# Norms issued behind their own tile's products, attention paced with weights, and new priorities in a list-scheduled two-layer decoder trunk

## The chip, the cores and the metric

The kernel runs on the 8 cores of one Trainium2 chip. Each core computes two of the 16 sequences, all cores run the same program, and they do not exchange data. The metric is the device time of the slowest core in microseconds (us). Within a core, TensorE (PE in the profile) does the matrix products, VectorE (DVE), ScalarE (ACT) and GpSimd (POOL) the element-wise work, and SyncE (SP) issues DMA transfers.

## The reference

`x` is 16 sequences of 2048 positions and 1024 channels. Cut to what matters:

```python
h = x
# layer 0
xn = rmsnorm(h, g0)
a, xb, gate_b, gate_c = split(xn @ ab_w_in)              # 512 columns each
mix = concat(pool_mixer(a), gate_b * conv3(gate_c * xb)) # windows 2/4/8/16; depthwise width 3
h = h + mix @ ab_w_out
h = h + square(relu(rmsnorm(h, g0m) @ w1_0)) @ w2_0      # 1024 -> 4096 -> 1024
# layer 1
xn = rmsnorm(h, g1)
u, v = split(gelu(xn @ cd_w_in[:, :1024]))
c = u * (W_s @ layernorm(v) + b_s)                       # causal, chunks of 128 positions
q, k, val = split(xn @ cd_w_in[:, 1024:])                # 8 heads of 64
z = q @ k.T / 8                                          # strictly causal
d = (sigmoid(z) * suffix_product(1 - sigmoid(z))) @ val  # stick-breaking, no softmax
h = h + concat(c, d) @ cd_w_out
h = h + square(relu(rmsnorm(h, g1m) @ w1_1)) @ w2_1
out = rmsnorm(h, gf)                                     # rmsnorm: h / sqrt(mean(h*h) + eps) * g
```

## The kernel before

**Tiles and stages.** Activations lie transposed, channels on partitions. A unit is 1024 positions of a sequence, in two halves t = 0, 1 of 512. F(s,u), for unit u of sequence s, is layer 0: an input projection of 16 weight blocks, pooling and convolution, an output projection of 8 blocks, an MLP of 64. M(s,u) is the first part of layer 1: gating (V, then U) and the projections to values, keys and queries. S(s,u) is the rest of it: output projection, MLP, final norm. The order is F(0,0) M(0,0) F(0,1) M(0,1) S(0,0) F(1,0) M(1,0) F(1,1) M(1,1) S(0,1) S(1,0) S(1,1).

**Groups.** A *group* (line 627) is eight products 128x512 that add up in one of three PSUM banks; another instruction then empties the bank: `evac_h` (line 701) adds it to the residual h on VectorE and squares the sum on ScalarE into the buffer X_45; in an MLP's first layer (W1) ScalarE does relu in the bank and then the square out of it. An MLP has four quarters: W1, W2, W1, W2.

**A norm** (line 640) of one half sums the eight squared tiles by eight products with a matrix of ones (in the profile `ps<-X_45,cbs`), in a first part of six when six tiles are squared and a second of two. ScalarE then does Ln (L651) and Exp (L655), and VectorE eight normalisations of 128x512 (L665), which write over the squares in X_45. The next stage's products read those. The norms after an output projection are spawned when all its 16 groups have been issued, those after layer 0's MLP when that MLP has been issued. `prefetch_x` (line 718) loads, squares and normalises the next unit's x into a second buffer, X_44, during the MLP before it.

**Attention** (lines 1161 to 1252) runs beside the other stages. An *item*, a query block of 128 by up to 512 keys, is two score products (L1206) into one of two pairs of PSUM banks, a sigmoid on ScalarE, two VectorE scans (L1217), a copy of the carry to the next item of the chain (L1225), a GpSimd difference (L1231) and a transposing transfer (L1244, Wk<-Wq) on SP's queue. After four items, eight value products follow (L1275). Items are released in proportion to `main_t`, the count of main products issued, over a window `win` set in `build`.

**Weights.** A ring of ten blocks is loaded on GpSimd's queue in the order that `block_order` lists (line 556). The first use of a block loads and converts f32; `keep_block` (line 595) then stores a bf16 copy from SP's queue, which later uses load. This falls on F(0,0), M(0,0) and the 72 blocks of S(0,0), the first tail pass.

**What sets the order.** All work is written as fibers that yield instructions, pool requests and conditions; a planner puts them in a fixed order per engine before the kernel runs. It takes the instruction with the smallest modelled start plus two biases, so a negative bias is an urgency:

```python
r = f.req
st = S.ready(r)
k = (st + f.bias + r.bias, f.n)
```

An engine then runs its instructions in that order. `hcount` makes an output projection wait until all eight tiles of a half's h are being loaded. `finbusy` holds a half while its final norm still uses mix as staging; the input groups of F wait for it.

## Time and profile before

| | us |
|---|---|
| median of 3 runs (lowest, highest) | 3035.44 (3034.34, 3356.67) |
| the profiled execution's own time | 3030.56 |
| its span on the slowest core (all cores) | 3029.0 (2994.9 to 3029.0) |
| TensorE busy | 2859.8 (94%) |
| VectorE, ScalarE, GpSimd busy | 1413.3, 1411.9, 1180.1 |

The profile is of one execution on its slowest core; times count from the start of the span. The clock column is TensorE's granted clock as a share of full speed, the mean over a stretch. The wait that the profile names ahead of an instruction is what ended the engine's idle time.

### The profile page before, as it was taken

What the parts mean: (1) busy time and instruction counts of PE and PEld (TensorE: products, weight loads), DVE (VectorE), ACT (ScalarE), POOL (GpSimd) and SP (SyncE); (2) the same over time, 40 slices, a digit from 0 to 9 for tenths busy, and PEclk for the clock granted to TensorE, in tenths of its full rate; (3) what the DMA queues carried; (4) which work ended last, traced back from release to release, by engine and by line L of the source; (5) the groups of instructions that cost most, each with busy time, mean ns of one, the idle gap of its engine ahead of it and who ended that gap; (6) DMA issues with size and microseconds to landing.
All of it is one profiled execution on the core that took longest, in us unless ns stands there. A gap on an engine that the chain in (4) does not pass through costs nothing.

```text
span 3029.0 us, 43342 instructions; the slowest of 8 cores (2994.9 to 3029.0 us)
## 1 busy us (share of the span) xinstructions
PE 2859.8 (94%) x13365; PEld 1215.2 (40%) x13365; DVE 1413.3 (47%) x1671; ACT 1411.9 (47%) x2398; POOL 1180.1 (39%) x1685
## 2 busy tenths in 40 slices
PE   8999989999989899899998999998999989999998
PEld 3344433344433334334343334443344434443443
DVE  3510237443435344883755472433555574644002
ACT  2344243556446344356454345444564556453442
POOL 4211136343333344653644543433355435641110
PEclk9999999999999899899999999999999989999999
DMA  7778972455867997754676253565356584755222
GB/s 160 174 171 181 195 201 72 122 114 126 200 175 121 158 174 151 189 134 107 147 165 183 73 108 96 118 145 174 79 117 125 101 219 109 135 113 171 83 77 84
DMA packets 456912, 420.18 MB, mean 139 GB/s; under 512 B 310256, under 2 KB 334960, under 8 KB 456688
## 3 DMA queue, kind: packets, MB, share of 16 engines
q1 hardware_dynamic: 387424, 228.46, 32.5%
q0 software_dynamic: 69264, 188.95, 29.1%
q8 instruction: 114, 1.87, 0.3%
q14 instruction: 110, 0.90, 0.1%
HBM read 304.20 MB, written 89.13 MB: 130 GB/s over the span
## 4 chain that ended last, share of the span: by engine, by line
PE 80%; DVE 6%; DMA 4%; POOL 3%; issue 3%; ACT 3%; SPq 1%; DVEq 0%; POOLq 0%; ACTq 0%
PE ps L550 76%; PE ps L1206 3%; DVE X_45 L665 2%; PE ps L1275 2%; DVE P L1217 1%; DMA Wk<-Wq 1%; DMA ring<-wblk 1%; POOL Wq L1231 1%; DMA h<-xT 1%; POOL ps_77 L934 1%; POOL ps_74 L934 1%; SPq L1244 0%; SPq L543 0%; DMA stg<-xT 0%; ACT ms L655 0%
## 5 line engine op out<-in xcount | busy, mean ns | idle before, releaser
L550 PE MATMUL ps<-X_45,ring 128*128 128x512 bf16 x4864 | 1107.0, 384 | 22.3 <-DVE X_45 L665 20.8
L540 ACT ACTIVATE ps<-ps 128x512 f32<-128x512 f32 (+3 forms) x832 | 575.5, 697 | 554.6 <-PE ps L550 323.6
L550 PEld LDWEIGHTS ps<-X_45,ring 128*128 128x128 bf16 x4864 | 469.6, 99 | 617.7 <-issue 90.1
L1231 POOL TENSOR_TENSOR Wq<-P 128x1022 bf16<-128x1022 f32 (+2 forms) x320 | 527.3, 1648 | 421.2 <-DVE P L1217 401.7
L550 PE MATMUL ps<-mix,ring 128*128 128x512 bf16 x2816 | 659.1, 380 | 3.9 <-DVE mix L905 3.0
L1217 DVE TENSOR_TENSOR_SCAN P<-ps,carry,cbs 128x512 f32<-128x512 f32 x384 | 486.7, 1276 | 244.5 <-ACT ps L540 233.4
L583 POOL DMA_DIRECT2D ring<-wbf x540 | 296.3, 550 | 778.6 <-PE ps L550 699.0
L706 DVE TENSOR_TENSOR h<-ps,h 128x512 f32<-128x512 f32 x384 | 263.2, 687 | 626.5 <-PE ps L550 623.2
L550 PE MATMUL ps<-ffB,ring 128*128 128x512 bf16 x2048 | 483.8, 379 | 0.0
L1217 DVE TENSOR_TENSOR_SCAN P<-ps,cbs 128x128 f32<-128x128 f32 (+3 forms) x256 | 208.1, 819 | 508.7 <-ACT ps L540 496.6
L550 PEld LDWEIGHTS ps<-mix,ring 128*128 128x128 bf16 x2816 | 262.1, 98 | 337.0 <-issue 44.2
L540 ACT ACTIVATE X_45<-h 128x512 bf16<-128x512 f32 x256 | 160.7, 628 | 393.1 <-DVE h L706 392.9
L550 PE MATMUL ps<-X_44,ring 128*128 128x512 bf16 x1280 | 297.9, 389 | 12.4 <-DVE X_44 L665 5.8
L550 PEld LDWEIGHTS ps<-ffB,ring 128*128 128x128 bf16 x2048 | 200.4, 98 | 241.7
L583 POOL DMA_DIRECT2D ring<-wblk x180 | 98.2, 553 | 368.8 <-PE ps L550 336.5
L550 PEld LDWEIGHTS ps<-X_44,ring 128*128 128x128 bf16 x1280 | 123.7, 100 | 170.8 <-issue 38.5
L540 ACT ACTIVATE mix<-ps 128x512 bf16<-128x512 f32 x288 | 171.8, 597 | 33.2 <-PE ps L550 7.6
L540 ACT ACTIVATE ffB<-ps 128x512 bf16<-128x512 f32 x256 | 152.8, 597 | 23.9 <-ACT ps L540 0.4
L665 DVE SCALAR_TENSOR_TENSOR X_45<-h,cfs,ms 128x512 bf16<-128x512 f32 x192 | 141.3, 807 | 31.2 <-ACT ms L655 31.2
L550 PE MATMUL ps<-ring,X_45 128*128 128x512 bf16 x512 | 127.6, 399 | 27.6 <-DVE X_45 L665 14.5
L1206 PE MATMUL ps<-kT,qT 64*128 64x512 bf16 (+3 forms) x640 | 112.1, 359 | 17.9 <-DVE P L1217 17.8
L1225 ACT ACTIVATE carry<-P 128x2 f32<-128x2 f32 x192 | 37.9, 199 | 125.7 <-DVE P L1217 124.8
(112 smaller groups left out, 1331.3 us busy)
## 6 DMA issues: line engine op xcount, KB each, us to landing
ring<-wbf POOLq DMA_DIRECT2D x540, 256.0 KB, 3.9
ring<-wblk POOLq DMA_DIRECT2D x180, 256.0 KB, 6.9
wbf<-ring SPq DMA_DIRECT2D x180, 256.0 KB, 5.4
stg<-xT SPq DMA_DIRECT2D x96, 256.0 KB, 4.6
h<-xT SPq DMA_DIRECT2D x64, 256.0 KB, 7.0
hsp<-h SPq DMA_DIRECT2D x64, 256.0 KB, 5.0
h<-hsp SPq DMA_DIRECT2D x64, 256.0 KB, 7.0
oT<-mixf SPq DMA_DIRECT2D x32, 256.0 KB, 7.1
```

The costliest lines, as they stand in the source:

```text
L540: return Req("act", lambda e: e.activation(out=out, in_=in_, func=func, **kw), reads, writes, dur, bias=bias)
L550: ins = pe.matmul(out, lhsT=l, rhs=r, start=(first and i == 0), stop=(last and i == n - 1), skip_group_check=True)
L583: yield Req("pool", (lambda slot, b, src: lambda e: e.dma_start(out=self.ring[:, slot, :], in_=src[b]))(slot, b, src), ([self.Lwbf[b]] if ...
L665: yield Req("dve", lambda e: e.scalar_tensor_tensor(out=X[:, c, ts], in0=self.h[:, c, ts], scalar=g, in1=m, op0=ALU.mult, op1=ALU.mult), [ ...
L706: yield Req("dve", lambda e: e.tensor_tensor(out=self.h[:, c, ts], in0=self.bank(bk), in1=self.h[:, c, ts], op=ALU.add), [], [self.Lbank[b ...
L934: yield Req("pool", (lambda src, d, b0: lambda e: e.tensor_tensor(out=S1[:, b0:528][:, ::-1], in0=src[:, b0:528][:, ::-1], in1=src[:, b0 - ...
L1206: ins = pe.matmul(zt[:, h * 512:h * 512 + w], lhsT=self.qT[hp, a, il * 128:(il + 1) * 128], rhs=self.kT[hp, a, k0:k0 + w], start=True, sto ...
L1217: yield Req("dve", (lambda h: lambda e: e.tensor_tensor_scan(out=P[:, h, 0:w][:, ::-1], data0=zt[:, h * 512:h * 512 + w][:, ::-1], data1=f ...
L1225: yield Req("act", lambda e: e.activation(out=self.carry[:, cy, :], in_=P[:, :, 0:1].rearrange("p h o -> p (h o)"), func=AF.Copy), [LP], [ ...
L1231: yield Req("pool", lambda e: e.tensor_tensor(out=W3[:, :, 0:w - 1], in0=P[:, :, 1:w], in1=P[:, :, 0:w - 1], op=ALU.subtract), [LP], [LWq] ...
L1275: ins = pe.matmul(av[h * 64:(h + 1) * 64, r0 * 128:512], lhsT=lhsT, rhs=rhs, start=(first and j == 0), stop=(c == 0 and j == 3), skip_grou ...
```

## The change

1. *Norms.* `out_proj` spawns the norms of both halves before its groups, and `stage_F` those of layer 0's MLP before the MLP, so that a norm can stand in the order as soon as its tiles are squared.
2. *Stage M.* The order V, U, values, K, Q becomes V, U, K, values, Q, in the code and in `block_order`. K and Q take one block at a time, V and values four.
3. *Pacing.* Items are released by `pace_t`, which counts a group in F's input projection as 0.4 and in S's output projection as 0.2 of a full one; the windows in `build` are shortened to match.
4. *Biases.* Ln and Exp -0.7, normalisations -1.0, `evac_h` -1.2, sigmoid -0.3, carry copy -1.0; an attention item's fiber 0.0 instead of 0.4, the final norm's -0.6 instead of 0.1.
5. *Conditions.* h loads are counted per tile (`hload`); `finbusy` is asked by the two instructions that write mix, not by the input groups.
6. `keep_block` is unchanged: S(0,0) stores the copies of its 72 blocks as before.

The diff, cut to its core; the lines that begin with # name the place:

```diff
+PACE = 0.4
+PACEO = 0.2
     # block_order, kind "M"
-                seq(B_V, 20)
+                seq(B_V, 8)
+                seq(B_K, 4)
+                seq(B_VV, 4)
+                seq(B_Q, 4)
...
     # group
         self.main_t += n
+        self.pace_t += n * self.pace_w
...
     # norm: Ln and Exp
-            [self.Lcf], [self.Lms[ms], self.Lbank[bk]], 1.9)
+            [self.Lcf], [self.Lms[ms], self.Lbank[bk]], 1.9, bias=-0.7)
...
     # to_X: X_45 <- h * g * m
-                [self.Lh[c][t], Lm, self.Lcf], [LX[c][t]], 0.75)
+                [self.Lh[c][t], Lm, self.Lcf], [LX[c][t]], 0.75, bias=-1.0)
...
     # evac_h: h <- bank + h
-                      [], [self.Lbank[bk], self.Lh[c][t]], 0.70)
+                      [], [self.Lbank[bk], self.Lh[c][t]], 0.70, bias=-1.2)
...
     # chain_conv gb, and chain_pool ahead of its ACTIVATE mix<-ps
-            yield lambda: "y" in st
+            yield lambda: "y" in st and t not in self.finbusy
...
     # stage_F
+        self.pace_w = PACE
         for i in range(4):
...
-                yield lambda: t not in self.finbusy
...
+        self.pace_w = 1.0
         self.free_x(n)
-        yield from self.out_proj("F", s, u, self.mix, self.Lmix)
         nd = set()
+        yield from self.out_proj("F", s, u, self.mix, self.Lmix, 8, nd)
         ev2 = [[0], [0]]
-        for t in range(2):
-            self.M.spawn(self.norm_h(self.evo[t], t, 8, self.to_X(t, 1), nd), -0.2)
...
-        yield from self.mlp(0, 8, nd, ev2, then)
...
         for t in range(2):
             self.M.spawn(self.norm_h(ev2[t], t, 16, dst(t), nd2), -0.2)
+        yield from self.mlp(0, 8, nd, ev2, then)
...
     # out_proj
+        evo = [[0], [0]]
+        for t in range(2):
+            self.M.spawn(self.norm_h(evo[t], t, gcol, self.to_X(t, 1), nd), -0.2)
         for t in range(2):
-            yield lambda: (self.mixn[t] == 8 if kind == "F" else (s, u, t) in self.mready) and \
-                self.hcount.get((kind, s, u, t)) == 8
+            yield lambda: self.mixn[t] == 8 if kind == "F" else (s, u, t) in self.mready
             for c in range(8):
+                yield lambda: (kind, s, u, t, c) in self.hload
...
     # stage_M
+        yield from heads(self.kT, self.LkT, u * UT)
         sl = yield from self.take(4)
         for n in range(8):                      # the eight V groups
...
-        for which in range(2):                  # K, then Q
+        yield from heads(self.qT, self.LqT, 0)
...
     # attention
-            yield lambda: self.pace_free or self.main_t >= pace[0] + need * pace[1]
+            yield lambda: self.pace_free or self.pace_t >= pace[0] + need * pace[1]
-            self.M.spawn(self.att_item(s, u, x), 0.4)
+            self.M.spawn(self.att_item(s, u, x), 0.0)
     # att_item: sigmoid bias -0.3, carry copy bias -1.0
...
     # stage_S
+        self.pace_w = PACEO
+        yield from self.out_proj("S", s, u, *src, 24, nd)
+        self.pace_w = 1.0
-            self.M.spawn(self.norm_h(self.evo[t], t, 24, self.to_X(t, 1), nd), -0.2)
...
-            self.M.spawn(fin(t), 0.1)
+            self.M.spawn(fin(t), -0.6)
...
     # build
-        tF, tM, tS = 88 * 16, 20 * 16, 72 * 16
+        tF, tM, tS = (72 + 16 * PACE) * 16, 20 * 16, (64 + 8 * PACEO) * 16
```

Three places in the order of the engines. An `order` row is an engine's next instructions: line, operation, output<-inputs, tile, count. L550 and L552 are the same line before and after, and so are L1206 and L1214, L1057 and L1064, L540 and L542, L651 and L657, L655 and L661.

TensorE at the end of F(0,1)'s output projection (`ps<-mix,ring`) and the start of its MLP (`ps<-X_45,ring`); the norm products are `ps<-X_45,cbs`. Before:

```order
L550 MATMUL ps<-mix,ring 128x512 x24
L1206 MATMUL ps<-kT,qT 128x384 x2
L550 MATMUL ps<-mix,ring 128x512 x16
L550 MATMUL ps<-X_45,cbs 128x512 x16
L1275 MATMUL ps<-Wk,V 64x512 x8
L550 MATMUL ps<-X_45,ring 128x512 x8
L1206 MATMUL ps<-kT,qT 128x512 x2
L550 MATMUL ps<-X_45,ring 128x512 x40
```

And now:

```order
L552 MATMUL ps<-mix,ring 128x512 x24
L552 MATMUL ps<-X_45,cbs 128x512 x6
L552 MATMUL ps<-mix,ring 128x512 x16
L552 MATMUL ps<-X_45,cbs 128x512 x2
L552 MATMUL ps<-mix,ring 128x512 x8
L1214 MATMUL ps<-kT,qT 128x512 x2
L552 MATMUL ps<-mix,ring 128x512 x40
L552 MATMUL ps<-X_45,cbs 128x512 x6
L552 MATMUL ps<-mix,ring 128x512 x8
L552 MATMUL ps<-X_45,ring 128x512 x4
L552 MATMUL ps<-X_45,cbs 128x512 x2
L552 MATMUL ps<-X_45,ring 128x512 x4
```

The first half's norm products now stand among the second half's groups, and the second half's last two behind four products of the MLP.

TensorE at the start of M(0,0): last groups of the MLP (`ps<-mix,ring` and `ps<-ffB,ring`), norms, V (`ps<-ring,X_45`), U (`ps<-X_45,ring`), gating products (`ps<-wmt,vn`). Before:

```order
L550 MATMUL ps<-mix,ring 128x512 x8
L550 MATMUL ps<-ffB,ring 128x512 x8
L550 MATMUL ps<-X_45,cbs 128x512 x16
L550 MATMUL ps<-ring,X_45 128x512 x32
L550 MATMUL ps<-X_45,ring 128x512 x8
L1057 MATMUL ps<-wmt,vn_79 128x128 x4
L1057 MATMUL ps<-wmt,vn_81 128x128 x4
L550 MATMUL ps<-X_45,ring 128x512 x8
L1057 MATMUL ps<-wmt,vn_83 128x128 x4
L1057 MATMUL ps<-wmt,vn_85 128x128 x4
L550 MATMUL ps<-X_45,ring 128x512 x16
L550 MATMUL ps<-ring,X_45 128x512 x32
```

And now:

```order
L552 MATMUL ps<-X_45,cbs 128x512 x6
L552 MATMUL ps<-mix,ring 128x512 x8
L552 MATMUL ps<-ffB,ring 128x512 x8
L552 MATMUL ps<-ring,X_45 128x512 x4
L552 MATMUL ps<-X_45,cbs 128x512 x2
L552 MATMUL ps<-ring,X_45 128x512 x28
L552 MATMUL ps<-X_45,ring 128x512 x32
L1064 MATMUL ps<-wmt,vn_79 128x128 x4
L1064 MATMUL ps<-wmt,vn_81 128x128 x4
L1064 MATMUL ps<-wmt,vn_83 128x128 x4
L1064 MATMUL ps<-wmt,vn_85 128x128 x4
L552 MATMUL ps<-ring,X_45 128x512 x32
```

The first half's gating products stood between its U groups; now they follow its four U groups in one piece.

ScalarE at the end of F(1,0)'s output projection and the start of its MLP: squares (`X_45<-h`), Ln (`ms<-ps,cfs`), Exp (`ms<-ms`), sigmoids (`ps<-ps` of 128x1024 and 128x2x384), squares of the next x (`X_44<-stg`), and of the MLP's first layer relu (`ps<-ps` of 128x512) and square (`mix<-ps`). Before:

```order
L651 ACTIVATE ms<-ps,cfs 128x512
L655 ACTIVATE ms<-ms 128x512
L651 ACTIVATE ms<-ps,cfs 128x512
L655 ACTIVATE ms<-ms 128x512
L1225 ACTIVATE carry<-P 128x2
L540 ACTIVATE ps<-ps 128x2x384
L540 ACTIVATE ps<-ps 128x1024
L540 ACTIVATE X_44<-stg 128x512 x3
L540 ACTIVATE ps<-ps 128x512
L540 ACTIVATE mix<-ps 128x512
L540 ACTIVATE ps<-ps 128x512
L540 ACTIVATE mix<-ps 128x512
```

And now:

```order
L1233 ACTIVATE carry<-P 128x2
L657 ACTIVATE ms<-ps,cfs 128x512
L1233 ACTIVATE carry<-P 128x2
L661 ACTIVATE ms<-ms 128x512
L542 ACTIVATE ps<-ps 128x1024 x2
L542 ACTIVATE ps<-ps 128x512
L542 ACTIVATE mix<-ps 128x512
L542 ACTIVATE ps<-ps 128x512
L542 ACTIVATE mix<-ps 128x512
L657 ACTIVATE ms<-ps,cfs 128x512
L542 ACTIVATE ps<-ps 128x512
L542 ACTIVATE mix<-ps 128x512
```

Before, Ln and Exp of both halves stood in one piece ahead of the MLP; now only the second half's are there, with a copy of a carry between, and the Ln that follows among the MLP's evacuations is that of the next x, whose squares now come earlier.

## Rows read from the trace of the kernel before

**Rows 1.** The page's head and its part 1

```profile
span 3029.0 us, 43342 instructions; the slowest of 8 cores (2994.9 to 3029.0 us)
...
PE 2859.8 (94%) x13365; PEld 1215.2 (40%) x13365; DVE 1413.3 (47%) x1671; ACT 1411.9 (47%) x2398; POOL 1180.1 (39%) x1685
```

**Rows 2.** Waits of TensorE: us in total, times, longest

```profile
PE ps L550 <- DVE X_45 L665: 35.3, 76, 2.1
PE ps L1275 <- DMA Wk<-Wq: 18.1, 2, 13.9
```

**Rows 3.** Timeline of TensorE, F(0,1): start us, us, instruction, count [idle before]

```profile
561.34 3.62 PE L550 MATMUL ps<-X_45,cbs 128*128 128x512 bf16 x16
...
567.02 0.38 PE L550 MATMUL ps<-X_45,ring 128*128 128x512 bf16 x1 [1.07 <-DVE X_45 L665]
567.68 0.38 PE L550 MATMUL ps<-X_45,ring 128*128 128x512 bf16 x1 [0.29 <-DVE X_45 L665]
...
598.68 31.25 PE L550 MATMUL ps<-X_45,ring 128*128 128x512 bf16 x144
```

**Rows 4.** Windows: length; busy us (count) of PE, PEld, DVE, ACT, POOL; clock, DMA

```profile
131.60:155.75 24.15, 21.66 (x89) 8.80 (x88) 11.39 (x17) 12.67 (x21) 0.53 (x1) 0.93 0.46 123
...
2171.39:2199.48 28.09, 24.44 (x104) 9.04 (x103) 19.69 (x24) 17.20 (x27) 9.19 (x9) 0.88 0.30 60
...
364.68:418.19 53.51, 38.87 (x178) 15.64 (x176) 36.33 (x54) 27.28 (x56) 22.73 (x34) 0.94 0.84 205
...
2048.98:2097.54 48.56, 36.60 (x178) 15.73 (x177) 28.61 (x48) 26.19 (x55) 22.68 (x33) 0.96 0.44 137
461.57:531.56 69.99, 63.25 (x300) 26.15 (x299) 55.83 (x65) 25.09 (x41) 51.73 (x84) 1.00 0.29 71
1227.20:1311.99 84.79, 69.99 (x314) 27.94 (x313) 77.37 (x79) 30.89 (x50) 61.87 (x99) 0.90 0.63 165
...
2442.29:2488.97 46.68, 37.78 (x169) 15.54 (x167) 33.95 (x40) 25.38 (x40) 19.20 (x24) 0.89 1.02 262
945.33:1028.69 83.36, 67.92 (x290) 27.18 (x291) 26.11 (x31) 45.15 (x77) 20.62 (x29) 0.86 0.94 148
...
2311.17:2372.16 60.99, 60.99 (x293) 25.73 (x292) 16.96 (x16) 43.46 (x75) 23.71 (x34) 1.00 0.47 108
```

**Rows 5.** Timeline of all engines around the start of M(0,1)

```profile
816.19 3.62 PE L550 MATMUL ps<-X_45,cbs 128*128 128x512 bf16 x16
...
817.25 0.63 ACT L540 ACTIVATE X_45<-h 128x512 bf16<-128x512 f32 x1 [3.43 <-DVE h L706]
...
819.69 5.39 DVE L665 SCALAR_TENSOR_TENSOR X_45<-h,cfs,ms 128x512 bf16<-128x512 f32 x8 [2.54 <-ACT ms L655]
...
839.06 7.75 DVE L665 SCALAR_TENSOR_TENSOR X_45<-h,cfs,ms 128x512 bf16<-128x512 f32 x7
...
840.99 1.61 POOL L1067 TENSOR_TENSOR vt_82<-vt_82,sbias 128x512 f32<-128x512 f32 x1 [0.73 <-ACT vt_82 L1063]
...
867.92 12.46 PE L550 MATMUL ps<-ring,X_45 128*128 128x512 bf16 x57 [2.66 <-DMA ring<-wbf]
```

**Rows 6.** Groups by line and shape: count | busy us, mean ns | idle

```profile
L1231 POOL TENSOR_TENSOR Wq<-P 128x1022 bf16<-128x1022 f32 x224 | 426.4, 1904 | 342.6 <-DVE P L1217 340.6 <-DMA Wk<-Wq 1.1 <-issue 0.2
L540 ACT ACTIVATE ps<-ps 128x512 f32<-128x512 f32 x544 | 316.5, 582 | 340.7 <-PE ps L550 323.6 <-PE ps L1206 16.3
...
L540 ACT ACTIVATE ps<-ps 128x1024 f32<-128x1024 f32 x224 | 224.6, 1009 | 158.0 <-PE ps L1206 157.9
...
L1225 ACT ACTIVATE carry<-P 128x2 f32<-128x2 f32 x192 | 37.9, 199 | 125.7 <-DVE P L1217 124.8
...
L540 ACT ACT_TABLE_LOAD x24 | 30.8, 1283 | 6.7 <-PE ps L550 5.0 <-PE ps L1206 1.4
```

**Rows 7.** Line L1244, the transposes of the attention weights

```profile
DMA to landing us min/median/max: 2.3/4.4/23.2
```

**Rows 8.** Timeline of TensorE in S(0,0)

```profile
1017.41 1.92 PE L1275 MATMUL ps<-Wk,V 128*64 128x512 bf16 x8 [13.86 <-DMA Wk<-Wq]
```

More of the change, by code:

```diff
@@ L652, in norm @@
                                           bias=self.cf[:, 60:61]),
-            [self.Lcf], [self.Lms[ms], self.Lbank[bk]], 1.9)
+            [self.Lcf], [self.Lms[ms], self.Lbank[bk]], 1.9, bias=-0.7)
         self.banks.free(bk)
-        yield Req("act", lambda e: e.activation(out=m, in_=m, func=AF.Exp, scale=-0.5), [], [self.Lms[ms]], 0.63)
+        yield Req("act", lambda e: e.activation(out=m, in_=m, func=AF.Exp, scale=-0.5), [], [self.Lms[ms]], 0.63, bias=-0.7)
         for c in range(8):
@@ L752, in start_x @@
             ts = slice(t * TT, (t + 1) * TT)
-            self.hcount[("F", 0, 0, t)] = 8
+            self.hload.update(("F", 0, 0, t, c) for c in range(8))
             ev = [0]
@@ L784, in load_h_chunk @@
             yield self.load_h(self.hsp, self.Lhsp, s, u, t, c)
-        k = (kind, s, u, t)
-        self.hcount[k] = self.hcount.get(k, 0) + 1
+        self.hload.add((kind, s, u, t, c))
     def free_x(self, n):
@@ L952, in evac @@
                           bias=-1.0, slack=1.0)
+            yield lambda: t not in self.finbusy
             yield Req("act", lambda e: e.activation(out=self.mix[:, g, ts], in_=self.bank(b2), func=AF.Copy,
@@ L1133, in stage_M, with heads @@
         yield from self.need_attention(2 * s + u)
+        def heads(dst, Ldst, d0):
+            for a in range(4):
+                sl = yield from self.take(1)
+                for t in range(2):
+                    ts = slice(t * TT, (t + 1) * TT)
+                    ev = copy_evac(dst[:, a, d0 + t * TT:d0 + (t + 1) * TT], [Ldst[a][d0 // TT + t]], "act")
+                    yield from self.group(self.wpairs(sl[0], X, ts), [self.Lring[sl[0]]] + [LX[k][t] for k in range(8)], ev)
+                self.release(sl[0])
+        yield from heads(self.kT, self.LkT, u * UT)
         sl = yield from self.take(4)
@@ L1140, in stage_M @@
             self.release(x)
-        for which in range(2):
-            for a in range(4):
-                sl = yield from self.take(1)
-                for t in range(2):
-                    ts = slice(t * TT, (t + 1) * TT)
-                    gs = slice(u * UT + t * TT, u * UT + (t + 1) * TT)
-                    if which == 0:
-                        ev = copy_evac(self.kT[:, a, gs], [self.LkT[a][u * 2 + t]], "act")
-                    else:
-                        ev = copy_evac(self.qT[:, a, ts], [self.LqT[a][t]], "act")
-                    yield from self.group(self.wpairs(sl[0], X, ts), [self.Lring[sl[0]]] + [LX[k][t] for k in range(8)], ev)
-                self.release(sl[0])
+        yield from heads(self.qT, self.LqT, 0)
         self.M.spawn(self.attention(s, u), 0.4)
@@ L1179, in attention @@
         acc = 0.0
-        pace = (self.main_t, self.win[(s, u)], tot)
+        pace = (self.pace_t, self.win[(s, u)], tot)
         self.inflight = 0
@@ L1210, in att_item @@
         z3 = zt[:].rearrange("p (h n) -> p h n", h=2)[:, :, 0:w]
-        yield self.act(z3, z3, AF.Sigmoid, [], Lz, 2 * w, True, scale=-0.125)
+        yield self.act(z3, z3, AF.Sigmoid, [], Lz, 2 * w, True, bias=-0.3, scale=-0.125)
         if pv is not None:
@@ L1225, in att_item @@
             yield Req("act", lambda e: e.activation(out=self.carry[:, cy, :], in_=P[:, :, 0:1].rearrange("p h o -> p (h o)"),
-                                                    func=AF.Copy), [LP], [self.Lcarry[cy]], 0.2)
+                                                    func=AF.Copy), [LP], [self.Lcarry[cy]], 0.2, bias=-1.0)
         x["scanned"] = True
@@ L1309, in stage_S @@
         src = (self.mix, self.Lmix) if self.stages[n - 1][0] == "M" else (self.X[0], self.LX[0])
-        yield from self.out_proj("S", s, u, *src)
+        nd = set()
+        self.pace_w = PACEO
+        yield from self.out_proj("S", s, u, *src, 24, nd)
+        self.pace_w = 1.0
         if src[0] is self.X[0]:
             self.free_x(n)
-        nd = set()
         ev2 = [[0], [0]]
-        for t in range(2):
-            self.M.spawn(self.norm_h(self.evo[t], t, 24, self.to_X(t, 1), nd), -0.2)
         nx = self.hnext
@@ L1392, in build @@
         self.main_t = 0
+        self.pace_t = 0.0
+        self.pace_w = 1.0
         self.ffn = [0, 0]
@@ L1399, in build @@
         self.hnext = None
-        self.hcount = {}
+        self.hload = set()
         self.xloading = False
```

5 lines of the change are left out of this document (2 added, 3 removed).

## The prediction

> **What bounds the kernel now.** I read the page's head first: TensorE is busy for 94% of a span of 3029.0 us [rows 1]. Work can therefore become cheaper only where TensorE stands still or runs slowly, and the list of its waits says where: VectorE's normalised tiles X_45 (35.3 us, 76 times), then the transposed attention weights (18.1) [rows 2]. The timeline shows the form of the first. After an output projection come 16 norm products in one piece, then a wait of 1.07 us, then single products 0.66 us apart, as each 128x512 piece of X_45 is written; undisturbed, 144 products take 31.25 us, or 0.216 each [rows 3].
>
> Waits alone understate it, so I priced stretches, window by window [rows 4]: length less its full products at 0.216 us. Attention products in a stretch are cheaper than full ones, so I count them whole for the floor and at nothing for the ceiling.
> - *Output projection to MLP*, eight times, from the first norm product to the 65th MLP product. The first has 88 full products: 24.15 - 19.0 = 5.1 us lost. The dearest (start 2171.39) has 80 full and 24 of attention: 28.09 less 22.5 or 17.3, so 5.6 to 10.8. Counted so, the eight lose 41 to 67; I take 55.
> - *MLP to mixer stage M*, four times, from the norm products to the first product of the K, V or Q projections: 144 full products and 32 of a quarter's width are 32.8 us. The first loses 53.51 - 32.8 = 20.7, the last 48.56 - 32.8 = 15.8, all four 73.
> - *Input projections of F(0,1), F(1,0), F(1,1)*: 264 full products, 57.0 us. F(0,1) loses 5.2 to 13.0 (I take 9), F(1,1) is like it (8), F(1,0) loses 17.0 to 27.8 (22).
> - *Output projection of S(1,0)*: 46.68 us, 144 full products, 10.2 to 15.6 lost (13).
>
> The granted clock averages 0.88 in the dearest handoff and 0.90 in F(1,0)'s input: after such gaps part of the products run at the lower level (1.2 GHz). A whole quarter of an MLP without gaps holds 1.00 (2311.17) [rows 4]. The windows contain that loss, so it is not added again. Together these places lose 180 us.
>
> **The change, part by part.**
> *Norms behind their own products.* Count of instructions is unchanged; 12 pairs of norms move. The first half's norm now stands among the second half's products, and the second half's last two norm products stand four products into the next stage (the order rows). For the first half the whole chain is hidden by 6 groups of 8 products or more, 10.4 us. For the second half I read the chain where it is seen alone: from the end of the products (816.19) the last square ends at 817.88, 1.7 us later; the norm products took 8 x 0.216 of the 3.5 us to the first normalisation at 819.69, so Ln and Exp need 1.8; eight normalisations take 5.39 [rows 5]. That is 1.7 + 0.4 + 1.8 + 5.4 = 9.3 us, under the next 64 products' 13.8. What stays: TensorE takes its instructions in order, so the two norm products wait for that square: 1.7 - 4 x 0.216 = 0.8 us; and behind Ln and Exp ScalarE does a table load and a sigmoid (1.28 and 1.01 [rows 6]) before it empties the first bank, which I put at another 1.2. Left: 8 x 2 = 16 of 55, gain **39** (25 to 58). The eight h loads that each M norm lets go, and the final norm's stores, issue earlier on SP's queue; nobody on TensorE waits for them there.
> *M stage.* The same 0.8 us, then the four gating products of the first half stand behind all its U products (before: between them) and need four banks, of which three exist: the fourth waits for ScalarE's four scalings, and so does the next V group. From the rows' durations I count about 4 us there and 3 to 4 at the second half's gating products. The VectorE block of second-half normalisations that ran beside the gating (7.75 us for seven) is out of the way, and K, taken one block at a time, replaces V, which needed four blocks at once and cost a wait of 2.66 us on the ring [rows 5]. On POOL's queue the loads stand no earlier, but only K's third block waits for them, 6.9 us later than V did. Left: 9 each, 36 of 73, gain **37** (13 to 57).
> *Pacing.* Input projections of F now count 0.4, output projections of S 0.2. In the order, F(0,1)'s input has 5 attention items instead of 9, F(1,0)'s 7 instead of 12, S(1,0)'s output 2 instead of 7. VectorE was busy 77.37 of 84.79 us in F(1,0)'s input [rows 4], which I take for the reason of the loss; I halve it there: gain **19** (9 to 29). In S(1,0)'s output seven items become two; gain **9.5** (5 to 13).
> *Where the items go.* Mostly into the W1 quarters of the MLPs (each MLP is W1, W2, W1, W2): the order has 170 scores in them instead of 93, up to 17 in one (F(1,0)'s first). That quarter then asks of ScalarE 64 evacuations at 0.58 (37 us), 17 sigmoids (17), about 13 carries at 0.20 (3) and, as the norm of the next x tile falls into the same place, four table loads (5) and two norms' Ln and Exp (at most 1.8 each by the rows above, 4): 66 us, against 55.3 of products and some 8 of attention's. So this one quarter is ScalarE-bound by a few us; the others, with 11 to 16, ask up to about 60 of 62. In the row without loss (2311.17, nine scores) ScalarE asked 43.46 of 60.99. Cost **8** (0 to 40).
> *Tail pass.* S(0,0) still stores the weight copies. Its first quarter goes from 9 to 14 scores, and there the transposes landed up to 23.2 us late against a median of 4.4, one value product waiting 13.86 us [rows 7, 8]; that quarter lost 83.36 - 290 x 0.216 = 20.7 us at a DMA share of 0.94 [rows 4]. Cost **6** (-18 to +40).
> *At nothing:* loads of h counted per piece only relax a condition that no wait of TensorE names. The condition that the final norm has left mix moves from the input groups to the two writers of mix; a writer that waits keeps one of three banks, and the groups behind it stop after two more. I take nothing, since the final norms now rank ahead of all else there; without that cover it would be the rest of eight normalisations, 5.4 us, at the one place where F follows S.
>
> Sum: 39 + 37 + 19 + 9.5 - 8 - 6 = 90.5. The profiled execution took 3030.56, so 2940; the median of the runs shown is 3035.44, 4.9 above it, so **2944 us**.
>
> **A rule against it.** The seven normalisations beside GpSimd's additions (840.99) took 1.11 us each, the eight without 0.67 [rows 5]. With 1.11 the second half's chain is 3.9 + 8.9 = 12.8 us, still under 13.8, and the sum stands. If instead each of the eight waited out one whole GpSimd difference (1.90 us [rows 6]), the chain would be 3.9 + 5.4 + 15.2 = 24.5, 10.7 late in six handoffs that now have attention beside them: 64 us given back. The Trainium skill has such a rule ("SBUF — State Buffer", Who interferes with whom): a VectorE instruction with two SBUF inputs and a GpSimd one that reads SBUF exclude each other, and the later is fully blocked. The rows agree that there is a cost, and show 0.44 us of it.
>
> **Rivals.**
> 1. *The second half's normalisations late* (just worked out): 2944 + 64 = 3008. It begins to cost at 4.5 us, 0.56 per instruction. For: POOL's differences move into that stretch. Against: the order puts two or three scores beside them, so two or three differences, not eight.
> 2. *ScalarE paces the denser quarters.* If half of each of 170 sigmoids (1.01 us [rows 6]) delays a bank, 170 x 0.5 = 85 us less the 8 counted: about 3021. For: 66 us asked of a quarter of 63 in F(1,0). Against: three banks leave 3.5 us between a group's end and the need for its bank.
> 3. *Slower: value products wait in the tail pass.* S(0,0) holds 12 of them, TensorE takes them in order, and one such wait with its slow products cost about 15 us (the 20.7 less the 5.9 that the handoff in it loses by the same count). Six more give the whole gain back; all 12 give 2944 + 11 x 15 = 3109. For: more transposes in a quarter with a DMA share of 0.94. Against: the pass holds 53 scores instead of 51, so the load is shifted, not raised.
> 4. *More goes away:* the residues at their least and the 18.1 us of transpose waits too: about 2897.
>
> That the change does nothing is excluded by the order.
>
> **Numbers.** Forecast 0.56 (2915 to 2974); rival 4 0.15; rival 1 0.08; rival 2 0.09; rival 3 with six or more waits 0.06; two to four more waits (about 2990 to 3010) 0.06. A difference of 2%, 61 us, is about what a measurement of this kernel can tell from none: below 2975 is faster (0.71), up to 3096 the same (0.24), above slower (0.05). The range 2895 to 2997 leaves out the slow end of rivals 1 to 3.
>
> **What would show it.** Right: X_45 waits of TensorE under 12 us; the eight handoffs at most 3 us over their products; from M's first to its 129th full product near 39 us; F(1,0)'s input near 73; S(1,0)'s output near 36. Wrong: waits for ScalarE's emptied banks in the first MLP quarters, value products waiting for transposes more than twice in S(0,0), or that stretch of M over 44 us.

## The result, and the profile after

The changed kernel takes **2965.93 us** (median of 4 runs, 2964.73 to 2966.79) against 3034.34 for the kernel before in the same job: a ratio of 0.9773, 95% interval 0.9754 to 0.9792. The prediction was 2944 with 2895 to 2997 as its range, so the time lies inside, with 68 us gained where 90.5 had been summed. In some executions the cores of one die run at a lower granted clock and take longer; all times here are medians of the other executions, and the kernels without stores and with the late final norm, which have one of these each, have no ratio.

The page's head and part 1 of the kernel after, beside [rows 1]:

```profile
span 2964.9 us, 43355 instructions; the slowest of 8 cores (2927.3 to 2964.9 us)
...
PE 2836.3 (96%) x13361; PEld 1210.1 (41%) x13361; DVE 1401.7 (47%) x1671; ACT 1416.4 (48%) x2408; POOL 1180.4 (40%) x1685
```

TensorE's waits (us in total, times, longest), beside [rows 2]:

```profile
PE ps L552 <- DVE h L712: 17.6, 9, 5.0
PE ps L552 <- ACT X_45 L542: 15.2, 15, 4.1
PE ps L1283 <- DMA Wk<-Wq: 9.6, 3, 7.1
```

The 35.3 us of waits for normalised X_45 tiles are gone. What is left of the norm is its last two products, which wait for the last square (15 times). At the top stands a wait that the kernel before does not have: for a bank that is not emptied, because `evac_h` waits for h.

The handoff of F(0,1), where [rows 3] had a wait of 1.07 us and eight single products 0.66 apart:

```profile
543.55 1.75 PE L552 MATMUL ps<-X_45,cbs 128*128 128x512 bf16 x6
...
546.88 1.03 PE L552 MATMUL ps<-X_45,ring 128*128 128x512 bf16 x4
548.78 0.59 PE L552 MATMUL ps<-X_45,cbs 128*128 128x512 bf16 x2 [0.87 <-ACT X_45 L542]
549.21 1.03 PE L552 MATMUL ps<-X_45,ring 128*128 128x512 bf16 x4
```

The wait of 0.87 us is the 0.8 that the prediction worked out from the square's end; the MLP's first eight products run without any other. The windows that answer to [rows 4] have the same columns (length; busy us and count of PE, PEld, DVE, ACT, POOL; clock; DMA share; GB/s). They are, in this order: M(0,0) from its first product to K's first, the inputs of F(0,1) and F(1,0), S(1,0)'s output, and F(1,0)'s first W1 quarter:

```profile
362.90:402.20 39.30, 33.78 (x163) 15.15 (x162) 20.85 (x37) 22.48 (x50) 18.36 (x28) 0.92 0.80 214
444.80:513.90 69.10, 62.49 (x284) 26.09 (x283) 43.04 (x58) 21.15 (x35) 44.85 (x79) 0.98 0.22 63
1187.30:1267.60 80.30, 66.83 (x297) 27.00 (x296) 65.51 (x72) 25.72 (x41) 57.26 (x93) 0.96 0.68 194
2383.20:2428.20 45.00, 35.75 (x150) 14.26 (x149) 30.65 (x40) 20.00 (x30) 12.51 (x16) 0.92 1.00 262
1300.30:1380.60 80.30, 72.77 (x333) 28.48 (x332) 55.98 (x53) 61.87 (x104) 45.52 (x52) 0.94 0.69 132
```

To see where the 64 us between the two spans went, I counted every stretch of both traces alike: its length less its products at 0.216 us per 512 columns, attention's by their width. "Lost" is that difference, on each trace's slowest core.

| stretch | lost before | after | gained | forecast |
|---|---|---|---|---|
| eight handoffs with their first W1 quarter, without value products' waits | 55.7 | 36.4 | 19.3 | 39 - 8 |
| four M stages | 69.1 | 38.9 | 30.2 | 37 |
| inputs of F(0,1), F(1,0), F(1,1) | 34.2 | 36.6 | -2.4 | 19 |
| output of S(1,0) | 11.5 | 13.1 | -1.6 | 9.5 |
| waits of value products in S(0,0) | 18.1 | 9.6 | 8.5 | -6 |
| all else | 5.0 | -4.8 | 9.8 | 0 |
| sum | 193.6 | 129.8 | 63.8 | 90.5 |

(An attention product costs a little less than its width, so a stretch without gaps can come out below nothing. A stage M counts from its first product; the wait for the norm ahead of it, which the prediction counted with M, stands in "all else".)

### The profile page after: what moved, and what is told of

It reads as the page before. It is cut to its first block, busy times and chain, and to the rows that moved or that the text cites. A ratio compares the mean times of both kernels' runs of the same rounds, so it can differ in the third digit from the quotient of the medians.

```text
span 2964.9 us, 43355 instructions; the slowest of 8 cores (2927.3 to 2964.9 us)
## 1 busy us (share of the span) xinstructions
PE 2836.3 (96%) x13361; PEld 1210.1 (41%) x13361; DVE 1401.7 (47%) x1671; ACT 1416.4 (48%) x2408; POOL 1180.4 (40%) x1685
## 4 chain that ended last, share of the span: by engine, by line
PE 84%; DMA 3%; ACT 3%; DVE 3%; issue 3%; POOL 2%; SPq 2%; DVEq 0%; ACTq 0%; POOLq 0%
PE ps L552 79%; PE ps L1214 3%; PE ps L1283 2%; SPq L1252 1%; DMA Wk<-Wq 1%; DMA h<-hsp 1%; POOL ps_74 L939 1%; DMA h<-xT 1%; SPq L545 1%; DVE P L1225 1%; ACT ps L542 1%; DVE h L712 1%; DMA ring<-wblk 0%; ACT vt_80 L1070 0%; POOL ps_77 L939 0%
## 5 line engine op out<-in xcount | busy, mean ns | idle before, releaser
L552 PE MATMUL ps<-X_45,ring 128*128 128x512 bf16 x4864 | 1100.6, 382 | 6.2 <-ACT mix L542 5.4
L542 ACT ACTIVATE ps<-ps 128x512 f32<-128x512 f32 (+3 forms) x832 | 574.1, 697 | 533.4 <-PE ps L1214 289.3
L552 PEld LDWEIGHTS ps<-X_45,ring 128*128 128x128 bf16 x4864 | 463.1, 98 | 583.0 <-issue 71.5
L552 PE MATMUL ps<-mix,ring 128*128 128x512 bf16 x2816 | 659.9, 381 | 3.0 <-ACT ffB L542 1.1
L552 PE MATMUL ps<-ffB,ring 128*128 128x512 bf16 x2048 | 483.8, 379 | 0.0
L552 PEld LDWEIGHTS ps<-mix,ring 128*128 128x128 bf16 x2816 | 264.4, 98 | 337.3 <-issue 42.3
L542 ACT ACTIVATE X_45<-h 128x512 bf16<-128x512 f32 x256 | 159.2, 627 | 378.0 <-DVE h L712 377.6
L552 PE MATMUL ps<-X_44,ring 128*128 128x512 bf16 x1280 | 302.9, 392 | 31.2 <-DVE h L712 15.1
L552 PEld LDWEIGHTS ps<-ffB,ring 128*128 128x128 bf16 x2048 | 200.3, 98 | 241.7
L552 PEld LDWEIGHTS ps<-X_44,ring 128*128 128x128 bf16 x1280 | 124.5, 100 | 195.3 <-issue 65.6
L542 ACT ACTIVATE mix<-ps 128x512 bf16<-128x512 f32 x288 | 171.8, 597 | 49.9 <-PE ps L552 26.9
L542 ACT ACTIVATE ffB<-ps 128x512 bf16<-128x512 f32 x256 | 152.8, 597 | 23.0 <-ACT ps L542 0.7
L552 PE MATMUL ps<-ring,X_45 128*128 128x512 bf16 x512 | 114.7, 383 | 5.0 <-ACT vt_80 L1070 5.0
L1214 PE MATMUL ps<-kT,qT 64*128 64x512 bf16 (+3 forms) x640 | 112.7, 354 | 6.2 <-DVE P L1225 6.0
```

Source lines behind the costliest of these rows:

```text
L542: return Req("act", lambda e: e.activation(out=out, in_=in_, func=func, **kw), reads, writes, dur, bias=bias)
L552: ins = pe.matmul(out, lhsT=l, rhs=r, start=(first and i == 0), stop=(last and i == n - 1), skip_group_check=True)
L1214: ins = pe.matmul(zt[:, h * 512:h * 512 + w], lhsT=self.qT[hp, a, il * 128:(il + 1) * 128], rhs=self.kT[hp, a, k0:k0 + w], start=True, sto ...
```

## Experiments: the norms and the priorities

**Only the norms' place undone.**

```diff
     # out_proj: behind all groups, as before
-        for t in range(2):
-            self.M.spawn(self.norm_h(evo[t], t, gcol, self.to_X(t, 1), nd), -0.2)
         for t in range(2):
...
+        for t in range(2):
+            self.M.spawn(self.norm_h(evo[t], t, gcol, self.to_X(t, 1), nd), -0.2)
```

> The changed kernel with only the place of the norms undone: each norm is spawned behind all 16 groups of the output projection, and behind the whole MLP of layer 0; biases, stage M, pacing stay changed. Theory of the prediction: the norms' place carries the eight handoffs (39 us) and most of what stage M gained (X_45 waits of about 6 us in each of four stages, 24), so about 2966 + 60 = 3026 us, with waits of TensorE for X_45 from VectorE back above 25 us. Rival: the urgency biases do it, since a norm that starts late but is served first loses little: at most 2990.

Measured: 3003.41 us, ratio to before 0.9902 (0.9886 to 0.9919). The place of the norms is worth about 38 us inside the changed kernel, more than half of its gain. The waits for normalised tiles are back, though smaller than in [rows 2]; 5.8 of the 31.8 us is the first wait for x, which every kernel here has:

```profile
PE ps L552 <- DVE X L671: 31.8, 61, 5.8
```

By the count of the table the handoffs lose 23 us more. The expectation's second part fell: the M stages lose only 2.8 us each more, or 3.9 with the quarter ahead of them, where 6 had been expected. More than half of what M gained came from elsewhere (below).

**Only the norms' place changed, on the kernel before.** The edit is the reverse one.

> The kernel before with only the norms spawned ahead of their own groups; order of stage M, pacing, biases and conditions as before. Undoing this in the changed kernel cost 39 us. Theory: the place of the norms is worth about the same alone, 3033 less 35 to 45, about 2993, and TensorE's waits for normalised X_45 tiles fall from 35 us to under 12. Rival: without the urgency biases the norm's Ln, Exp and normalisations stand behind attention's scans and sigmoids, and half of it is lost: 3010 or more.

Measured: 3005.78, ratio 0.991 (0.9878 to 0.9942), about 26 us. Theory and rival were both half right. The waits for X_45 from VectorE are gone, and by the count of the table the stretches gain 59 us; but 32 are given back in one place that nobody had named. The last W2 quarter of S(1,0), in this kernel and, below it, in the changed one:

```profile
2621.20:2729.30 108.10, 75.08 (x361) 30.06 (x360) 75.99 (x76) 41.16 (x63) 55.30 (x61) 0.83 0.81 176
```

```profile
2623.80:2684.70 60.90, 60.90 (x291) 27.02 (x290) 20.85 (x27) 15.25 (x23) 14.39 (x21) 1.00 0.43 94
```

The attention of the last unit is late and has to be finished before S(1,1) can start, so TensorE waits for one item after the other. Two of those waits (idle before in brackets):

```profile
2702.53 0.61 PE L1205 MATMUL ps<-kT,qT 64*128 64x512 bf16 x2 [6.47 <-DVE P L1216]
...
2727.50 1.92 PE L1274 MATMUL ps<-Wk,V 128*64 128x512 bf16 x8 [9.59 <-DMA Wk<-Wq]
```

**All priorities undone, the rest as changed.**

```diff
-            [self.Lcf], [self.Lms[ms], self.Lbank[bk]], 1.9, bias=-0.7)
+            [self.Lcf], [self.Lms[ms], self.Lbank[bk]], 1.9)
...
-            self.M.spawn(self.att_item(s, u, x), 0.0)
+            self.M.spawn(self.att_item(s, u, x), 0.4)
...
-            self.M.spawn(fin(t), -0.6)
+            self.M.spawn(fin(t), 0.1)
```

> The changed kernel with all priorities of before (Ln, Exp, normalisation, evac_h, sigmoid, carry, attention items, final norm). Theory: the priorities are what the early norms need, above all where attention runs beside them, so 15 to 30 us go: 2980 to 2996, in the handoffs of F(0,1), F(1,1), S(0,1), S(1,0). Rival: the place of a norm decides alone and the rest is noise of the order: 2956 to 2972; S(1,0)'s and S(1,1)'s output projections then don't change either, because their h loads, not the final norms, are late.

Measured: 3005.16, ratio 0.9918 (0.9886 to 0.9949): about 40 us lost, more than expected and in other places. The stretches here are of core 0. The handoffs named there lose about what they do in the changed kernel (F(0,1) 0.8 against 3.4, S(0,1) 2.1 against 0.7). The loss is the same pile-up in S(1,0)'s last quarter:

```profile
2616.50:2724.60 108.10, 74.63 (x359) 30.19 (x358) 70.62 (x74) 40.03 (x61) 53.05 (x59) 0.84 0.75 173
```

A smaller one stands in M(1,0), ahead of which the second unit's attention has to end: it loses 30 us instead of 8.9. So the priorities together are worth as much as the norms' place, and without them attention does not keep up with its window. Two kernels with early norms and old priorities show the pile-up, and the kernel before, with late norms, does not (its same quarter loses nothing). My reading is that attention's items then rank behind everything and are left over; which of the priorities matters was not tried. S(1,0)'s output lost only 5.4 here; why is open (below).

## Experiments: pacing and the input projections

**Both weights at 1.0** (`PACE = 1.0`, `PACEO = 1.0`, which also restores the old windows).

> The changed kernel with both weights at 1.0 and so the windows of before: items are released evenly again. Theory of the prediction (VectorE's scans make the input projections long): F(0,1)'s input from 69.1 to about 74, F(1,0)'s from 80.3 to about 88, S(1,0)'s output longer by 8, the first W1 quarter of F(1,0) shorter by 7: about 2986 us. Rival: GpSimd's pooling additions pace the input projections and the h loads S(1,0)'s output, so the pacing is worth nothing there: inputs of F(0,1) and F(1,1) stay within 1.5 us of 69.1, the total between 2960 and 2972.

Measured: 2959.54, ratio 0.9767 (0.9744 to 0.9789). Taking the pacing out costs nothing; the time is 6 us lower, but the intervals overlap, and the mean over the cores is the same (2946.2 against 2946.8). F(0,1)'s input, with nine items again:

```profile
444.60:513.60 69.00, 63.23 (x301) 26.12 (x300) 54.99 (x65) 25.27 (x42) 52.05 (x83) 1.00 0.35 86
```

Against the row of after VectorE has 55 us of work instead of 43, and the stretch is 0.1 us shorter. VectorE's room is not what bounds it. What does, all engines in F(0,1)'s input of the changed kernel:

```profile
462.38 2.18 POOL L588 DMA_DIRECT2D ring<-wbf  x4
...
463.88 0.60 ACT L542 ACTIVATE pa_72<-ps 128x512 f32<-128x512 f32 x1 [1.03 <-PE ps L552]
...
466.10 1.04 POOL L939 TENSOR_TENSOR ps_74<-pa_72 128x518 f32<-128x518 f32 x1
...
467.29 2.23 POOL L939 TENSOR_TENSOR ps_74<-ps_74 128x516 f32<-128x516 f32 x2
...
469.60 1.46 POOL L1239 TENSOR_TENSOR Wq<-P 128x766 bf16<-128x766 f32 x1
469.62 1.98 DVE L948 SCALAR_TENSOR_TENSOR pb_73<-ps_74,pa_72 128x512 bf16<-128x512 f32 x1 [0.75 <-POOL ps_74 L939]
...
471.53 0.68 DVE L891 TENSOR_TENSOR cc_69<-ps,cy_68 128x512 f32<-128x512 f32 x1
...
472.35 0.59 PE L552 MATMUL ps<-pb_73,cbs 128*128 128x512 bf16 x1 [2.39 <-DVE cc_69 L891]
```

Read from the bottom: TensorE waits 2.39 us for a bank that L891 empties; in VectorE's order that stands behind the pooling's L948; that one waits for GpSimd's three additions. GpSimd began them 1.6 us after ScalarE had written their input (pa_72, done at 464.48), behind the issue of four weight loads and three small copies. So the chain runs through GpSimd. Not all of the 2.39 us is its additions, though: L948 took 1.98 us, with a GpSimd difference beside it, where its median is 0.69, and that alone is 1.29.

**The pooling additions on VectorE.**

```diff
-                yield Req("pool", (lambda src, d, b0: lambda e: e.tensor_tensor(
+                yield Req("dve", (lambda src, d, b0: lambda e: e.tensor_tensor(
```

> The changed kernel with the additions of the pooling mixer (20 in each F stage, 1.05 us each on GpSimd) issued to VectorE; nothing is left out. If GpSimd's chain of additions sets the pace of the input projections, F(0,1)'s and F(1,1)'s go from 69.1 to 62 to 65 us, F(0,0)'s from 75 to about 68, the total to about 2945. Rival (VectorE is what is short there): VectorE gets about 14 us more on 43 of 69, the inputs stay at 69 or get longer, the total is 2966 or more.

Measured: 2941.92, ratio 0.971 (0.968 to 0.974), faster than the changed kernel by some 20 us. F(0,1)'s input, with the same five items and without the one group of value products:

```profile
441.10:504.50 63.40, 60.02 (x277) 25.61 (x276) 53.48 (x75) 20.29 (x33) 23.35 (x54) 1.00 0.23 63
```

69.1 became 63.4 (F(1,1): 63.0; F(1,0): 80.3 to 73.5), with VectorE busier and GpSimd at half. By the count of the table F(0,1) loses 5.2 instead of 9.8, F(1,1) 4.7 instead of 9.7, and F(1,0) 13.3 instead of 17.0, there with three items in the order instead of seven. F(0,0)'s input ended only 2.7 us earlier, where 7 had been expected. So the additions on GpSimd made half of the loss in F(0,1) and F(1,1) and less elsewhere. Whether by their length or by what GpSimd's work does to VectorE's instructions beside it, the run does not tell.

**Both at once.**

> Pooling additions on VectorE and both pacing weights 1.0. Theory from the runs so far: pacing is worth nothing in any stage, so the two gains add up: 2942 less 6, about 2936. Rival: VectorE has 55 of 63 us in the inputs now, so with nine items instead of five there it becomes what is late, the inputs of F(0,1) and F(1,1) go from 63 to 67 us and more, and the total to 2950 or more.

Measured: 2949.17, ratio 0.9714 (0.9676 to 0.9753). The gains did not add up. Inputs of 63.8 and 63.4: the rival's 67 did not come either, but the rival was not put to the test, because the planner set six items into these inputs and not nine. By the intervals the kernel cannot be told from the one with the additions alone. By the mean over the cores all its executions (2930.8 to 2941.8) lie above all of that one's (2921.7 to 2928.3), so with the additions out of the way the pacing may be worth some 10 us; where, I did not find out.

## Experiments: the tail pass S(0,0)

On the core shown value products wait 9.6 us there; on core 0 of the same execution one wait is this:

```profile
1034.17 1.92 PE L1283 MATMUL ps<-Wk,V 128*64 128x512 bf16 x8 [18.33 <-DMA Wk<-Wq]
```

On core 1 one wait is 20.6, and core 6 has none. These waits go with a part of the spread of the cores, 2927.3 to 2964.9, and not with all of it: core 6 is the shortest, but core 5, the longest, has 9.6 us of them, and core 1, with 21.9, spans 2947.1.

**No weight copies in the tail passes.** S(0,0) stores none; the later passes load f32.

```diff
-            if b not in self.Lwbf:
+            if b not in self.Lwbf and b < B_L1OUT:
```

> The changed kernel without the bf16 copies of the 72 blocks of the tail passes: S(0,0) stores nothing, and S(0,1), S(1,0), S(1,1) load f32 again, twice the bytes. Theory: the stores in S(0,0) are what makes transposes of attention weights land late there, so its value products no longer wait (9.6 us on the slowest core, 24.6 on core 0) and the cores lie closer together than the 37 us of now: about 2950. Rival: the f32 loads alone fill the DMA engines and the waits stay; or the doubled loads of the later passes make TensorE wait for ring blocks, most of all in S(1,0)'s output projection: 2966 or more.

Measured: 2980.19, ratio 0.9825 (0.981 to 0.9839), slower than the changed kernel by 14. Both sides held in part. On the slowest core S(0,0) still has a value wait of 6.5 us without a single store. But over the eight cores these waits fall from 0 to 24.6 us (mean 13.4) to 0.6 to 6.5 (mean 2.1), so most of the lateness in S(0,0) did come with the stores. What is lost is lost later, as the rival had it. On the slowest core S(0,1), which had no such wait, loses 14.5 in one quarter, where the DMA share is 1.17. The longest wait stands there:

```profile
2233.23 1.92 PE L1283 MATMUL ps<-Wk,V 128*64 128x512 bf16 x8 [10.83 <-DMA Wk<-Wq]
```

Core 7 has 11.0 us of such waits in S(0,1), the other six at most 2.1. S(1,0)'s output loses 20.1 instead of 13.1. So f32 loads without stores can make transposes late too.

**The copies made earlier**, DRAM to DRAM from GpSimd's queue, by a fiber that the code has and did not use:

```diff
+        M.spawn(self.convert(B_L1OUT, 72, 1728, 2300), 0.5)
...
     # convert
+            if b in self.Lwbf:
+                continue
```

> The changed kernel with the 72 weight copies of the tail passes made ahead of need, DRAM to DRAM from GpSimd's queue, spread evenly from the start of F(0,1) to past the middle of S(0,0), which then loads bf16. Theory: the waits for late transposes in S(0,0) (9.6 us on the slowest core, 0 to 24.6 on the others) come from its DMA load, which falls from 0.94 of the engines; they go, the cores' spans lie within 15 us, about 2950. Rival: the same bytes now make transposes late in F(0,1), or 72 more DMA issues lengthen GpSimd's pooling chain there: 2963 or more.

Measured: 2966.05, ratio 0.977 (0.9729 to 0.981), no gain. The first half of the theory is right: on the slowest core S(0,0)'s four quarters lose nothing and no value product waits there, and no core has one of more than 5.1 us there. The rest of it fell, nearly as the rival had it. The last W2 quarter of F(0,1) loses 15.2, and only 3.5 of that is a value product's wait. 8.3 us are norm products that wait for squares; on ScalarE these stand behind the squares of the next x, for whose loads ScalarE waited up to 7.6 us at a time. M(0,1) loses 21.1 instead of 9.9, with a wait for attention's output ahead of S(0,0):

```profile
793.92 0.63 ACT L542 ACTIVATE X<-stg 128x512 bf16<-128x512 f32 x1 [6.57 <-DMA stg<-xT]
...
795.22 2.36 PE L552 MATMUL ps<-X,cbs 128*128 128x512 bf16 x6 [4.26 <-ACT X L542]
...
PE ps L552 <- DMA mix<-dsp: 10.7, 1, 10.7
```

**Value products later in the order**, on top of the additions on VectorE:

```diff
-                  bias=-1.0, slack=4.0)
+                  bias=-1.0, slack=16.0 if (s, u) == (0, 1) else 4.0)
```

> Pooling additions on VectorE, and the value products of the attention that runs beside S(0,0) and F(1,0) planned 12 us further behind their transposes (slack 16 instead of 4), with other products in between. Theory: the wait in S(0,0) is one of order, since TensorE takes its instructions in turn; a transpose that lands 20 us after its issue costs nothing when its products stand later. Then the single wait of 12 to 14 us on three cores is gone or under 4, and the slowest core falls from 2938 to about 2926. Rival: the buffers of weights are held longer, the next transposes go out later and land as late against their products as before, or the attention is late at the end of F(1,0): 2938 or more.

Measured: **2931.93 us**, ratio to before 0.965 (0.9622 to 0.9677), faster than both kernels. No core has a wait for Wk<-Wq in its list any more. The transposes of S(0,0) (here on core 7) land as late as ever; in the changed kernel the same line reads 2.3/6.4/19.6:

```profile
DMA to landing us min/median/max: 2.3/6.9/20.0
```

The wait was one of order, as the theory says: with other products in between, a landing after 20 us stops no value product. But the mean over the cores of these executions is 2923.8 us, against 2924.2 with the additions alone. What fell is the distance of the slowest core from that mean, from about 20 us to about 10. The average core lost elsewhere what it no longer waits here. On core 7, S(0,0)'s last quarter now has a wait of 3.6 us for a scan.

## Experiments: S(1,0)'s output, and stage M

**No stores of S(0,1)'s output**, whose part of the result is left out.

```diff
     # to_out, around the store of oT
+            if (s, u) != (0, 1):
...
```

> The changed kernel without the 16 stores of the output of S(0,1), whose part of the result is left out. S(1,0)'s output projection follows at once and waits for h loads (13.1 us lost in 45.0, DMA share 1.00). Theory: the DMA engines are full there with stores, h loads and weights, so without the stores it loses at most 7 us and is 39 us long or less. Rival: the final norm's own work on VectorE and SP's queue of transposes hold the loads up, so it still loses 10 or more. The rest of the kernel is as it is, so the total falls by that difference alone.

The profiled execution took 2952.62 us. S(1,0)'s output:

```profile
2386.90:2419.40 32.50, 32.47 (x153) 13.95 (x150) 25.14 (x35) 19.30 (x28) 9.04 (x13) 1.00 0.71 202
```

45.0 became 32.5 and the 13.1 us lost became 0.5; the DMA share went from 1.00 to 0.71. In the changed kernel the same place reads (all engines):

```profile
2382.48 6.02 SPq L545 DMA_DIRECT2D h<-hsp  x7
...
2391.77 0.69 DVE L712 TENSOR_TENSOR h<-ps,h 128x512 f32<-128x512 f32 x1 [6.02 <-DMA h<-hsp]
...
2392.61 1.67 PE L552 MATMUL ps<-X_44,ring 128*128 128x512 bf16 x7 [3.00 <-DVE h L712]
```

The h tile is late, `evac_h` waits, the bank is not emptied, TensorE stops. The stores cause it, by their bytes, by their places in SP's queue, or by VectorE's waits for staging; the run takes away all three and does not tell them apart.

**Only the final norm's priority undone** (0.1 instead of -0.6).

> The changed kernel with only the final norm's priority undone (0.1 instead of -0.6). With all priorities undone S(1,0)'s output projection lost 5.4 us instead of 13.1, and without the stores of S(0,1) 0.5. Theory: the hurried final norm puts its stores ahead of the h loads in SP's queue and in the DMA engines, so with 0.1 the output projections of S(1,0) and S(1,1) lose 5 to 8 and 2 to 5 us instead of 13.1 and 9.9: about 2955. Rival: it is the attention items' priority, whose transposes stand before the h loads on SP: both stay within 2 us, total 2961 to 2971.

Measured in one execution: 2976.92 us, 11 more than the changed kernel and above the 2971 of the rival. In the profile core 0 loses 11.4 in S(1,0)'s output and 13.2 in S(1,1)'s, and 23.7 instead of 17.1 in F(1,0)'s input. The theory fell: these outputs lose 11.4 and 13.2, not 5 to 8 and 2 to 5. In S(1,0)'s output the waits for h halve, from 8.7 us to 4.3, but a norm's wait for a square (5.7) takes their place. The rival holds for S(1,0) alone, and its cause, the priority of the attention items, has no run of its own; nor has the condition that now lets h loads be counted per tile. Why S(1,0) lost only 5.4 with all priorities undone stays open; that kernel's attention was behind there, with its work moved to the next quarter.

**Stage M in its old order.**

> The changed kernel with stage M in the order V, U, values, K, Q again. Theory: the order saves the wait of the values' first product for the fourth ring block (2.7 to 4.1 us in each of four stages before), so the total is about 2966 + 12 = 2978 and each stage M is 2.5 to 4 us longer. Rival: the values find their blocks once the norm no longer holds the stage up, or other waits take the place: within 5 us of 2966.

Measured: 2979.04, ratio 0.9837 (0.9795 to 0.9878), 13 us slower. By stages the four M lose 7 us more, and the wait for the ring is back (8.7 us in four waits, 0.3 in the changed kernel). On the slowest core the value waits of S(0,0), which differ from core to core, are 23.8 us, and that would be the rest. The order is worth about 7, not 12.

## Why the prediction was right, and where its terms were not

*Handoffs.* Right in six of eight. In those where nothing else changed (all but F(1,0) and S(1,1)) the loss went from 41.4 to 15.5, 2.6 on average, where 2 had been forecast. F(1,0) and S(1,1) lose 10 and 11, where at most 3 had been named. The second half's chain was never late: no wait for a normalised X_45 tile is left, so rival 1 is out, although single normalisations took up to 2.28 us.

*Denser quarters.* The size (8) was right, the cause only in part. F(1,0)'s first quarter loses 9.9 instead of 3.0, more of it in waits of score products for the scans (4.2) than in waits for ScalarE's emptied banks (2.8). The other quarters lost nothing, so rival 2 is out.

*Stage M.* Right. Counted from the norm products on, as the prediction did, the four stages lost 73 before and lose 35.5 now, 8.9 each where 9 had been worked out: a gain of 37, as forecast. First product to K's first is 38.4 to 39.3 us, as named. The parts are only partly known: undoing the norms' place gives back about 16 and the order about 7, while the norms' place alone, on the kernel before, takes the table's row only from 69.1 to 66.4. For the rest there is no run of its own; without the priorities three of the four stages lose about the same.

*Pacing: the step that failed.* "VectorE was busy 77.37 of 84.79 us in F(1,0)'s input [rows 4], which I take for the reason of the loss" was an inference from a share of busy time. Both terms (19 and 9.5) came out at about nothing, and undoing the pacing costs nothing. F(1,0)'s input took 80.3 us where 73 had been named, S(1,0)'s output 45.0 where 36 had. In the inputs of F(0,1) and F(1,1) about half of the loss came from the additions on GpSimd, although GpSimd's busy share in F(0,1), 51.73 of 69.99 [rows 4], was lower than VectorE's. In S(1,0)'s output TensorE waited before for scans, and now for h. The two lines are the largest waits of that window, before and after:

```profile
PE ps L1206 <- DVE P L1217: 6.9, 3, 2.8
```

```profile
PE ps L552 <- DVE h L712: 8.7, 3, 4.2
```

The h loads, next in line, took the place of the scans. With the weights at 1.0 four items stand there instead of two, and no product waits for a scan either.

*At nothing.* That "nobody on TensorE waits for them there" was wrong for the final norm. Hurried, it waits for its staging buffer's store and holds VectorE, where the last `evac_h` stands behind it:

```profile
1191.08 0.75 DVE L691 SCALAR_TENSOR_TENSOR stg<-h,cfs,ms 128x512 f32<-128x512 f32 x1 [5.57 <-DMA oT<-stg]
1191.75 0.68 DVE L712 TENSOR_TENSOR h<-ps,h 128x512 f32<-128x512 f32 x1
...
1193.30 1.01 PE L552 MATMUL ps<-X_45,cbs 128*128 128x512 bf16 x2 [4.10 <-ACT X_45 L542]
```

Still, without that priority the stretch loses more (23.7). The h loads counted per piece, put at nothing because they "only relax a condition that no wait of TensorE names", are now what its largest wait goes back to (17.6 us); whether the looser condition makes them late was not tried. The price of the late h in S(1,1)'s output is 4.8 more than before.

*Tail pass.* Forecast 6 lost, measured 8.5 gained, inside the -18 to +40 given. Rival 3 has the right mechanism: three value products wait on the core shown, and more than two had been named as a sign of being wrong, but they are short there. How long they are differs by core, from nothing to 24.6 us in all. On the slowest core this came out 14 better than forecast and made up for nearly half of the 32 that pacing missed; that is luck.

*Priorities* had no term of their own in the sum, and are worth about 40 us: they keep the attention from piling up before S(1,1). The forecast held because it took the order as built, with them in it.

## What to carry to other kernels

A busy share does not name what paces a stretch: follow one wait back, engine by engine, to the one that was never idle in between, before a term is priced. When a wait is taken away, ask what would have come second; here h loads stood right behind the scans. Where a consumer stands in an in-order queue behind a transfer of varying length, moving the consumer later took one number and no bytes, where two attempts to change the transfers gained nothing. Look at the mean over the cores as well as at the slowest: here the later consumers made the cores alike and the average core no faster.

## What the runs showed of the hardware

- A transpose landed after 2.3 to 20.0 us within one stretch, with DMA shares of 0.60 to 1.16, and the longest wait for one in S(0,0) ran from nothing to 20.6 us over the cores of one execution. With bytes taken out of that stretch the waits there fell (from a mean of 13.4 us to 2.1 without the stores), and others came in the stretches that got the bytes.
- VectorE's L948 took 1.98 us with a GpSimd difference of 1.46 beside it, and has a median of 0.69. That is 1.29 longer, nearly the whole difference, where [rows 5] showed 0.44. By the Trainium skill ("SBUF — State Buffer", Who interferes with whom) the pair of ports that the two engines share is an exclusive lock, and this row agrees with it. It makes such places dearer by about one GpSimd instruction, not whole stretches.
- The additions took 0.69 us each on VectorE against 1.05 on GpSimd.
